# The inverse of the delta rule's triangular matrix: matrix squarings replaced by a 16-wide recurrence, halves of the heads staggered

## The reference

```python
def gdn_chunk_scan(q, k, v, log_a, beta, s0):
    g = jnp.cumsum(log_a, axis=2)
    diff = g[:, :, :, None] - g[:, :, None, :]
    a_mat = jnp.einsum("bclhd,bcshd->bclsh", k, k) * beta[:, :, :, None] * masked_exp(diff, strict)
    lhs = jnp.moveaxis(a_mat, -1, 2) + jnp.eye(CHUNK, dtype=a_mat.dtype)
    rhs = jnp.concatenate([v * beta[..., None], k * (beta * jnp.exp(g))[..., None]], -1)
    sol = lax.linalg.triangular_solve(lhs, jnp.moveaxis(rhs, 3, 2), left_side=True, lower=True, unit_diagonal=True)
    u, w = sol[..., :dv], sol[..., dv:]
    ...
    def step(s, inp):
        v_new = u_c - jnp.einsum("bhlk,bhkv->bhlv", w_c, s)
        o = jnp.einsum("bhlk,bhkv->bhlv", qg_c, s) + jnp.einsum("bhls,bhsv->bhlv", qk_c, v_new)
        s = s * dec_c[..., None, None] + jnp.einsum("bhlk,bhlv->bhkv", kd_c, v_new)
```

## Time and profile before

| | us |
|---|---|
| median of 3 executions | 1867.92 (1863.32 to 1871.38) |
| the profiled execution: its own time | 1869.31 |
| its span | 1867.6 |
| TensorE busy in the span | 1708.2 (91%) |
| VectorE busy | 684.6 (37%) |
| ScalarE busy | 435.7 (23%) |
| GpSimd busy | 213.2 (11%) |

### The profile page before, as it was taken

How to read it: one execution, slowest core, us unless ns; L and a number is a source line. 1 busy time by engine, 2 the same in 40 slices (tenths; PEclk the granted TensorE clock), 3 DMA queues, 4 the chain that set the end, 5 groups by cost and what they waited for, 6 DMA issues and landing times.

```text
span 1867.6 us, 25449 instructions
## 1 busy us (share of the span) xinstructions
PE 1708.2 (91%) x10656; PEld 1209.9 (65%) x10656; DVE 684.6 (37%) x1404; ACT 435.7 (23%) x889; POOL 213.2 (11%) x190
## 2 busy tenths in 40 slices
PE   7999999999888879999999899899989989699996
PEld 3558555456666547767766588666978874488842
DVE  2107113335434353323233377665355450400003
ACT  1010454013111123323332231322333430000000
POOL 2000000020000012221212100011342320100000
PEclk9999999998988889999999899999999999799998
DMA  7444335723999888979989434224121222244340
GB/s 242 163 148 143 128 125 190 251 103 135 372 394 350 326 317 343 416 318 365 415 340 393 171 137 148 90 91 176 62 91 46 91 91 90 90 138 178 123 155 38
DMA packets 124295, 372.69 MB, mean 200 GB/s; under 512 B 10523, under 2 KB 26517, under 8 KB 107413
## 3 DMA queue, kind: packets, MB, share of 16 engines
q1 hardware_dynamic: 118245, 361.12, 51.6%
q0 software_dynamic: 1568, 8.39, 1.2%
q10 hardware_dynamic: 4368, 1.54, 0.4%
HBM read 369.98 MB, written 1.05 MB: 199 GB/s over the span
## 4 chain that ended last, share of the span: by engine, by line
PE 77%; DMA 13%; DVE 7%; ACT 1%; issue 1%; SPq 0%; DVEq 0%; ACTq 0%
PE psum L1976 49%; PE psum L571 10%; DMA ring<-in_w_down 4%; PE psum L1775 4%; DMA ring<-in_w_up 4%; DMA ring<-in_w_in 4%; PE psum L1970 3%; PE psum L1816 2%; PE psum L1759 2%; PE psum L1797 1%; PE psum L2093 1%; PE psum L768 1%; PE psum L2123 1%; PE psum L557 1%; DVE area L1180 1%
## 5 line engine op out<-in xcount | busy, mean ns | idle before, releaser
L1976 PE MATMUL psum<-area,ring 128*128 128x256 f32 x1984 | 457.7, 391 | 15.1 <-DMA ring<-in_w_in 14.1
L1976 PE MATMUL psum<-ring,area 128*128 128x512 f32 (+1 forms) x1040 | 452.5, 595 | 8.6 <-DMA ring<-in_w_proj_mem 2.4
L1976 PEld LDWEIGHTS psum<-area,ring 128*128 128x128 f32 x1984 | 386.1, 197 | 75.2 <-DMA ring<-in_w_in 18.1
L1976 PEld LDWEIGHTS psum<-ring,area 128*128 128x128 f32 x1040 | 198.9, 193 | 252.7 <-issue 251.7
L571 PEld LDWEIGHTS psum<-area 128*128 128x128 f32 x2304 | 269.7, 194 | 34.7 <-issue 19.1
L571 PE MATMUL psum<-area 128*128 128x128 f32 x2304 | 281.0, 280 | 10.6 <-DVE area L1180 10.4
L949 ACT ACTIVATE area<-psum 128x512 f32<-128x512 f32 x236 | 138.7, 597 | 243.7 <-PE psum L571 127.8
L2249 ACT ACTIVATE area<-psum 128x512 f32<-128x512 f32 x116 | 66.4, 599 | 460.9 <-PE psum L1976 362.2
L1970 PE MATMUL psum<-const,area 128*128 128x128 f32 x736 | 120.6, 294 | 52.0 <-DVE area L1490 14.8
L1970 PEld LDWEIGHTS psum<-const,area 128*128 128x128 f32 x736 | 90.5, 149 | 97.4 <-issue 23.0
L1775 PE MATMUL psum<-ring,area 128*32 128x256 f32 x2048 | 124.8, 388 | 12.5 <-DMA ring<-in_w_up 12.3
(11 more groups left out here) (304 smaller groups left out, 1346.5 us busy)
## 6 DMA issues: line engine op xcount, KB each, us to landing
ring<-in_w_gate SPq DMA_DIRECT2D x64, 1024.0 KB, 9.6
ring<-in_w_up SPq DMA_DIRECT2D x64, 1024.0 KB, 11.5
ring<-in_w_down SPq DMA_DIRECT2D x64, 1024.0 KB, 11.3
ring<-in_w_in SPq DMA_DIRECT2D x29, 2048.0 KB, 8.4
ring<-in_w_ada SPq DMA_DIRECT2D x12, 2048.0 KB, 8.1
ring<-in_w_in SPq DMA_DIRECT2D x13, 1024.0 KB, 7.5
ring<-in_w_out SPq DMA_DIRECT2D x6, 2048.0 KB, 8.5
ring<-in_w_ffn_gate SPq DMA_DIRECT2D x5, 2048.0 KB, 7.8
```

Source lines behind the costliest of these rows:

```text
L1976: last = nc.tensor.matmul(dst, lhs(k), rhs(k), start=first and k == 0, stop=final and k == count - 1)
```

## The change

The squarings go. For each half, VectorE cuts the diagonal 16-blocks out of A and compacts them to 16 columns (`rows`), GpSimd spreads these over a 16 by 16 grid (`spread`), TensorE multiplies by the block mask (`gRep`, two products 512 wide) so that every partition of a block holds the whole block (`rep`, copied out by ScalarE), and VectorE solves the block column by column: 15 pairs of linked instructions on 4n elements, n from 15 down to 1 (`solve`). The three levels now keep only the transposed inverse. The former `w` product and the second product of `v` become one product of keys and state (`gK`) that is subtracted from the values first. Decay rows (`gR` and `ssd_rows`) are transposes of the running sums in place of products with a triangular mask.

The two halves of four heads are now two streams. Half 0 is six phases (`STAGGER`) ahead of half 1, phases alternate, and the costs in `context_phases` are new ones.

```diff
+def staggered(first, second):
+    for _ in range(STAGGER):
+        yield "0 " + next(first)
+    while True:
+        phases = [("1 ", next(second, None)), ("0 ", next(first, None))]
...
-    gdn = [("rows", 3.1), ("gram", 1.9), ("AT", 1.2), ("P2", 3.8), ("X2", 5.7), ("X4", 3.8), ("X8", 1.9), ("XT0", 1.2),
...
+    costs = {"rows": 1.2, "gram": 1.0, "compact": 0.5, "rep": 1.8, "solve": 0.5, "X0": 1.6, "Y0": 1.0, "X1": 1.6, "Y1": 1.0,
+             "X2": 2.1, "Y2": 1.0, "v": 1.0, "S": 1.0}
...
         def gdn_pe(pe, m, h, open_tile, transposes):
-                four(("gR", m, h), lambda i: log_a[side][:, t, d, 16 + 4 * h + i:17 + 4 * h + i].to_broadcast([P, P]),
-                     lambda i: (upto, since)[d])
+            transposes(("gR", m, h), [cum[side][:, d, t, 16 + head:17 + head].to_broadcast([P, P]) for head in heads])
...
+            pe.wait_ge(s["spread_ready"], 2 * m + h + 1)
+            for i in range(2):
+                pair = slice(2 * i, 2 * i + 2)
+                nc.tensor.matmul(open_tile(("gRep", m, h, i)), blk16, b["spread"][:, pair, :, :].rearrange("p h i j -> p (h i j)"),
+                                 start=True, stop=True).then_inc(filled, 1)
+            yield "rep"
+            yield "solve"
             for lev in range(3):
+                if lev == 0:
+                    pe.wait_ge(s["XT_ready"], 2 * m + h + 1)
+                else:
+                    wait_drained(pe, ("gY", m, h, lev - 1))
+                transposes(("gX", m, h, lev), [b["XT"][:, i, :] for i in range(4)])
+                pe.wait_ge(s[f"levels_{h}"], 3 * m + lev + 1)
+                four(("gV", m, h, lev), lambda i: b["AL"][:, i, :], lambda i: b["XT"][:, i, :])
+                if ci and lev == 2:
+                    wait_drained(pe, ("gS", m - 2, h))
+                    four(("gK", m, h), lambda i: b["kT"][:, i, :], lambda i: state[:, 4 * h + i, :])
+                yield f"X{lev}"
+                four(("gY", m, h, lev), lambda i: b["X"][:, i, :], lambda i: b["VT"][:, i, :])
                 yield f"Y{lev}"
...
         def gdn_dve(eng, m, h, link, spread):
+            link(v.tensor_tensor(block, b["A"], blk16.unsqueeze(1).to_broadcast([P, 4, P]), ALU.mult))
+            v.tensor_reduce(rows, block.rearrange("p h (g j) -> p h j g", j=16), AX.X, ALU.add).then_inc(s["rows_ready"], 1)
+            yield "compact"
+            yield "rep"
+            link(v.tensor_copy(Y, unit_16.unsqueeze(1).to_broadcast([P, 4, 16])))
+            for i in range(2):
+                wait_drained(eng, ("gRep", m, h, i))
+            for j in (range(15), range(15, 0, -1))[d]:
+                left = (slice(j + 1, 16), slice(0, j))[d]
+                n = left.stop - left.start
+                link(v.tensor_tensor(tmp[:, :, 0:n], rep[:, :, left, j], Y[:, :, j:j + 1].to_broadcast([P, 4, n]), ALU.mult))
+                link(v.tensor_tensor(Y[:, :, left], Y[:, :, left], tmp[:, :, 0:n], ALU.subtract))
+            for i in range(4):
+                ins = v.tensor_tensor(b["XT"][:, i, :].rearrange("p (g j) -> p g j", j=16),
...
+            ins.then_inc(s["XT_ready"], 1)
+            yield "solve"
...
         def gdn_pool(eng, g, m, h):
+            eng.wait_ge(s["rows_ready"], 2 * m + h + 1)
+            for i in range(4):
+                ins = g.tensor_tensor(b["spread"][:, i, :, :], b["rows"][:, i, :].unsqueeze(1).to_broadcast([P, 16, 16]),
+                                      unit_16.unsqueeze(2).to_broadcast([P, 16, 16]), ALU.mult)
+            ins.then_inc(s["spread_ready"], 1)
+            yield "compact"
```

The decay products of the latent state space steps (`ssd_rows`):

```diff
-                        last = nc.tensor.matmul(dst[:, j * P:(j + 1) * P],
-                                                log_a[1][:, c - 2, d, 4 * q + j:4 * q + j + 1].to_broadcast([P, P]),
-                                                (upto, since)[d], start=True, stop=True)
+                        last = nc.tensor.transpose(dst[:, j * P:(j + 1) * P],
+                                                   cum[1][:, d, c - 2, 4 * q + j:4 * q + j + 1].to_broadcast([P, P]), ident)
```

More of the change, by code:

```diff
@@ L21 @@
 CTX_GAP = 3
+STAGGER = 6
 SLOTS = 6
@@ L122, in context_phases @@
     phases += [(f"ssd{m}", 1.8) for m in range(4)]
-    for m in range(4):
-        phases += [(f"{name} {m}", cost) for name, cost in gdn if name != "w" or m >= 2]
-    return phases
+    half = [f"{name} {m}" for m in range(4) for name in costs]
+    return phases + [(phase, costs[phase.split()[1]]) for phase in staggered(iter(half), iter(half))]
 def mixed_schedule():
@@ L347, in two_block_kernel, with delta_half @@
         ssd_gain = at(14336, D)
[L348 to L350 removed]
+        def delta_half(h, wide, spread_at, columns, small_at):
+            triangle, keys, block, decay = [place + 512 * h for place in columns]
+            wide, spread_at, small_at = wide + 1024 * h, spread_at + 1024 * h, small_at + 64 * h
+            return {"rep": at(wide, 4, 16, 16), "XT": at(wide, 4, P), "X": at(wide + 512, 4, P),
+                    "spread": at(spread_at, 4, 16, 16), "VT": at(spread_at, 4, P), "AL": at(spread_at + 512, 4, P),
+                    "A": at(triangle, 4, P), "kT": at(keys, 4, P), "block": at(block, 4, P), "QK": at(decay, 4, P),
+                    "rows": at(small_at, 4, 16), "Y": at(small_at + 128, 4, 16), "step": at(small_at + 256, 4, 16)}
+        delta = [[delta_half(h, 26592, 28640, (30688, 31712, 32736, 32736), 33760) for h in range(2)],
+                 [delta_half(h, 8192, 10240, (16000, 17024, 25216, 26240), 15360) for h in range(2)]]
+        unit_16 = stats[:, 24:40]
         o_tmp = [at(27264 + 512 * h, 4, P) for h in range(2)]
@@ L668, in gdn_pe @@
[L668 to L678 removed]
+            transposes(("gkT", m, h), [k_gdn[side][:, t, head * P:(head + 1) * P] for head in heads])
@@ L680, in context_channel_pe, with gdn_steps, of_half @@
+            if ci < 3:
+                pe.wait_ge(s["k_rest_ready"], 2 * m + h + 1)
+                four(("gS", m, h), lambda i: b["block"][:, i, :], lambda i: b["VT"][:, i, :])
+            yield "S"
+        def gdn_steps(steps, half):
+            def of_half(h):
+                for m in steps:
+                    for phase in half(m, h):
+                        yield f"{phase} {m}"
+            return staggered(of_half(0), of_half(1))
         def context_channel_pe(pe, n, open_tile, unit, product):
@@ L1206, in gdn_dve @@
-            for h in range(2):
-                wait_drained(eng, ("gKK", m, h))
-                negated(bb[h][4], bb[h][1], blk16).then_inc(s["n_ready"], 1)
-            for h in range(2 if side else 0):
+            for which, clip in (("A", ALU.max), ("QK", ALU.min))[:1 + side]:
+                src = four(("gR", m, h))
+                for i in range(4):
+                    ins = v.tensor_scalar(b[which][:, i, :], src[:, i, :],
+                                          cum[side][:, d, t, 16 + 4 * h + i:17 + 4 * h + i], 0.0, ALU.subtract, clip)
+                if which == "A" and side:
+                    ins.then_inc(s["gdn_clipped"], 1)
+                else:
+                    ins.then_inc(drain_of(("gR", m, h)), 1)
@@ L1236, in gdn_dve @@
-            if ci:
-                yield "w"
-            for h in range(2 if side else 0):
+            wait_drained(eng, ("gKK", m, h))
+            block, rows = b["block"], b["rows"]
+            link(v.tensor_tensor(block, b["A"], blk16.unsqueeze(1).to_broadcast([P, 4, P]), ALU.mult))
+            v.tensor_reduce(rows, block.rearrange("p h (g j) -> p h j g", j=16), AX.X, ALU.add).then_inc(s["rows_ready"], 1)
+            yield "compact"
+            yield "rep"
+            rep, Y, tmp = b["rep"], b["Y"], b["step"]
@@ new lines, in gdn_pool @@
+            for i in range(4):
+                ins = g.tensor_tensor(b["spread"][:, i, :, :], b["rows"][:, i, :].unsqueeze(1).to_broadcast([P, 16, 16]),
+                                      unit_16.unsqueeze(2).to_broadcast([P, 16, 16]), ALU.mult)
+            ins.then_inc(s["spread_ready"], 1)
+            yield "compact"
+            yield "rep"
+            wait_drained(eng, ("gKK", m, h))
+            level(0)
+            yield "solve"
+            level(1)
+            yield "X0"
+            yield "Y0"
@@ L1597, in context_pool @@
                 yield f"ssd{m}"
-            for m in range(4):
-                for phase in gdn_pool(eng, g, m, link):
-                    yield f"{phase} {m}"
+            for phase in gdn_steps(range(4), lambda m, h: gdn_pool(eng, g, m, h)):
+                yield phase
         def experts_pool():
@@ L2401, in _ @@
             eng.wait_ge(s["ident_ready"], 1)
+            link(v.tensor_reduce(unit_16, ident.rearrange("p (g j) -> p j g", j=16), AX.X, ALU.add))
             for i in range(2):
```

468 lines of the change are left out of this document (161 added, 307 removed).

## The result

The changed kernel takes 1931.0 us (median of 4 runs, 1926.6 to 1935.6) against 1865.6 us before (4 runs), a ratio of 1.035 with a 95% interval of 1.031 to 1.038. It is slower by 65 us; 1866 was forecast, and the range ended at 1898. The profiled execution has a span of 1927.7 us.

What follows compares the result with a forecast made beforehand. The chain ended on TensorE for 77% of the span and DMA for 13%. From 1869.3: -22 (experts), -7 (state space), +5 (latent), +18 (clock), +3 (GpSimd) = 1866.3, forecast as 1866 us; range 1836 to 1898.

Steps and rivals of the forecast that it cites:

- TensorE's work: Fewer product groups on TensorE: 58 us saved in the latent delta steps, 55 in the context steps.
- The recurrence: VectorE's block solve: 30 links of 0.23 us plus four writes, 7.8 us per half (ends 7.0 and 9.2).
- Experts' second half: Context delta steps beside expert loads: 22 of 45 us in question won, recurrences mostly covered by expert products and loads.
- The end of -5: Unfavourable end for the experts' second half: in-order VectorE holds the experts' own copies behind recurrences of 7.8 us.
- State space steps: 64 products become transposes, with some less waiting behind: -7 us (ends -8 and 0).
- Latent steps, clock at full, and the clock: Latent delta steps: 241 us against 236 (+5); half-speed work after two long waits per step adds +18.
- extras: Latent delta steps: 15 us added to the stage for other work that lengthens the new steps.
- GpSimd beside VectorE: GpSimd's first level mask falls on each latent recurrence: about 0.4 us, eight times, +3 (ends 0 and +10).
- The 0.4: Forecast cost in us to a VectorE recurrence of each GpSimd mask that falls on it.
- The covering streams: Rival, chance 0.30: the two halves' streams cover each other, the latent stage takes 229 us, time 1842 us.
- The low clock: Rival, chance 0.12: latent granted clock below about 0.65, TensorE's step path at half speed, 68 for 18, 1916 us.
- The experts' stage wins nothing: Rival, chance 0.16: DMA idle moves to stretches where TensorE waits for a recurrence; -2 instead of -22, 1886 us.

## Why the prediction was wrong, by its own steps

- *TensorE's work* (58 us saved in the latent part): right. Busy time fell by 25 only, but if each moment of it is counted with the clock granted then, it falls from 211 to 153 us, which is 58. The low clock accounts for 39 of the 192 us (5 before).
- *The recurrence* (7.8 us per half): right. The 30 links take 7.0 us (mean 0.225 and 0.193), the four writes 0.9.
- *Experts' second half* (-22, measured +24 over the whole stage): this step failed most. It said that the recurrence "mostly has expert products and loads beside it", one wait of 5 us excepted. TensorE waited twelve times in front of spreading and recurrence, 43.6 us. The gain was there (567.5 us with short recurrences and better costs, 568 with the full arithmetic, the recurrence in pieces and two phases more), so the failure isn't in the DMA's part of the argument but in the order: I worked out how much work there is beside the steps, not what stands right behind each recurrence on TensorE, nor that a planner that is told 0.5 us puts 0.5 us of experts there. 19 us are that, and some 24 the recurrences themselves: 591.8 - 567.5 when they are shortened, and as much (591.8 - 568) when they are cut in pieces, with the stagger and the phases changed too. Taken in the other order the two are 30 and 13.5. The end of -5 was no bound: it priced VectorE's held copies and no stop of TensorE.
- *State space steps* (-7, measured 0): the work went, the wait for VectorE grew. "Some less waiting behind" was wrong in sign (7.7 us before, 11.6 behind the transposes alone).
- *Latent steps, clock at full, and the clock* (+5 and +18, measured +45 together): 241 + 18 = 259 stand against 281. Idle time was forecast at 241 - 158 = 83 and measured at 90; the clock at 18, and it accounts for up to 34 (39 less the 5 of before). The order of the links was right at the step that I followed. The clock term was mis-sized: not only the waits for two recurrences in a step lower it but also those before the replications, of 2.9 us on average. The "extras" were too small as well, by 3 us at step 5.
- *GpSimd beside VectorE* (+3): small as forecast on the recurrences, four full collisions in the latent part and four in the experts' stage, but by another mechanism. 0.74 us in place of 0.26: the first link ends with the mask. The 0.4 came from the mean 1.08 of the earlier trace rows, which mixes masks of 0.68 us with others of 1.77 beside a mask of GpSimd. It is cheap here only because 0.6 of the mask's 1.27 us have passed by then.
- *The rivals.* The covering streams fell with the recurrences; it takes a broken recurrence to make them, and even then only in part (260). The low clock fell by its own point, 0.80 against 0.65. "The experts' stage wins nothing" named the right mechanism, with a price of 20 us for what cost 46 (24 lost where 22 were to be won).

What stays open: why the split recurrence leaves the latent part at 260. Its waits are spread over spreading, recurrence and levels, and no run takes one of these away alone. No order that was tried, with the full arithmetic, brought the latent part below 260, so how far a better order could go there isn't shown.

## What to carry to other kernels

Work that is moved from a busy engine to idle ones pays here only where something independent stands behind it in each engine's own order; read that from the rows behind each new wait, not from busy shares. A long chain of small instructions on an in-order engine is better cut into pieces with the other stream's work between them (34 us less in the experts' stage and 21 in the latent part, with the new stagger and costs), and a planner must be told its true length: the same arithmetic took 611 or 568 us here. Where two stages run the same routine with different cover, change it only where there is cover.

## What the runs showed of the hardware

In these traces a small VectorE instruction with two operands in SBUF that starts beside a GpSimd tensor_tensor ends within 0.1 us of that one's end: 0.74 us for 0.26 beside a mask of 1.27, and in the kernel with the split recurrence 2.28 for 0.22:

```profile
1414.24 2.35 POOL L1588 TENSOR_TENSOR area<-area,gdn_gain 128x1024 f32<-128x1024 f32 x1
...
1414.39 2.28 DVE L1185 TENSOR_TENSOR area<-area 128x60 f32<-128x60 f32 x1
```

A wide one, which takes 0.68 us alone, ends 0.54 us behind the mask (changed kernel):

```profile
1344.37 1.27 POOL L1491 TENSOR_TENSOR area<-area,const 128x512 f32<-128x512 f32 x1
1344.94 1.24 DVE L1167 TENSOR_TENSOR area<-area,const 128x512 f32<-128x512 f32 x1
```

The subtraction of a level (L1190), with one operand in PSUM, takes 0.68 us beside a mask too (at 1342.01, the mask from 1341.80 to 1343.08).

The Trainium skill ("SBUF — State Buffer", section "SBUF: two separate sides") calls the port pair that VectorE and GpSimd share an exclusive lock, held for the whole instruction, and not a split of bandwidth. These rows agree; my 0.4 us per mask would fit a split of bandwidth.

Idle float32 transposes ahead of a wait kept TensorE's clock at 2.4 GHz behind it in five of eight cases, products of about the same length in six, and neither in none (granted clock of the stage 0.88 and 0.87 against 0.80).
